# Two transformer blocks in full precision: the second block's mixing reordered with two heads in step, its context turned earlier, tables loaded ahead

## The chip, the core and the metric

One core of one Trainium2 chip runs the whole kernel. Its engines work side by side and wait for each other by semaphores: TensorE (PE, with its weight loads, PEld), VectorE (DVE), ScalarE (ACT), GpSimd (POOL) and SyncE (SP); the last two mainly issue DMAs here. The metric is the device time of one execution in microseconds (us); lower is better.

## The reference, cut to what matters

Two blocks of depth 2 follow each other on 256 latent tokens of width 1024. Each has its own 256 context tokens; the second block gets its own, `ctx_2`, so that these don't depend on the first block. The first block has feed-forwards, attentions and layer norms; its last feed-forward works on the 256 latent tokens alone. The second block's layer is (latent and context in layer 0; in layer 1 context only gives keys and values):

```
h  = rms_norm(x) * (1 + scale) + shift          # 512 tokens
p  = h @ w_in                                    # u, v, f, q-latent, kv-latent, k-rope: 1216 columns
ya = gelu(u) * (w_sgu @ (rms_norm(gelu(v)) * sgu_norm) + b_sgu)      # chunks of 128 tokens
yb = real(fft2(f))                                                    # over tokens and 64 channels
q  = rms_norm(rms_norm(pq) * q_lora_norm @ w_uq) * q_norm             # 4 heads of 128 + 64
k, v = from rms_norm(pkv) * kv_lora_norm @ w_ukv; k = rms_norm([k, k_rope]) * k_norm
q, k = rope(q), rope(k)                          # latent tokens
yc = softmax(q k^T / sqrt(192)) v                # latent: 512 keys; context: 256 keys
x  = x + gate * (concat(ya, yb, yc) @ w_out)
x  = x + gate2 * expert_choice_moe(...)          # 16 experts, 32 tokens each
```

## The kernel before, in words

Activations lie with channels on the 128 partitions and tokens along the free axis: `h` is 8 tiles of 128 x 512, latent tokens first. Large products are made of three products of reduced-precision halves: ACT copies a weight tile from `raw` to `whi` (L1308), DVE subtracts to get `wlo` (L1721), activations are split the same way into `xhi` and `xlo`, and PE multiplies hi by hi, lo by hi and hi by lo (L686 to L688, and L716 to L718 for the first three weight tiles of a stage, which take input tiles as they come). SP fetches weight tiles ("units") of 512 KB into a ring of four; ACT and DVE split three ahead. Small products are in full precision (`small_product`), two instructions each. Every engine runs its instructions in the order in which they are written; PSUM banks 0 to 7 are handed over by `acquire`, `filled`, `evacuated`. Banks 0 to 3 serve the products with units, 4 to 7 the rest.

The first block ends with layer 1's window attention (two heads in step; scores L906, turning of probabilities L933), an output projection, a layer norm and a feed-forward on 256 tokens. `layer_norm` and `inverse_root` sum squares on PE (L767), take the root on ACT (L1392, `square_root`) and the reciprocal on DVE (L1839), and spread it by PE (L774). The feed-forward's input goes DVE (L1869), ACT (L1356, L1361), DVE (L1756), the last two over all 512 columns. POOL streams modulation weights (`ride`, L2361) one feed-forward after the other, then waits until block 1 is done, loads `ctx_2` (L2401) and the small weights of the second block (L2411). PE turns `ctx_2` (L1036), DVE copies it to `h` (L2135).

A layer of the second block: squares (L1563), root, scaling, then ten tiles of input products in the order u, v, f, q, kv, k-rope, whose results ACT moves to `px` with gelu or copy (L1589). Then all the small work, one piece after the other on PE: sums of squares (L1065), turning of w_sgu (L1071), Fourier over channels (L1078), one reciprocal for three norms (L2164), Fourier over tokens (`fourier`, L1049), turning of v (L1094), the gate with its bias as a one-row product (L1103, L1104; DVE L2196), queries, keys, values (through L1023), sums over heads (L1023, `sq`), reciprocals (`inverse`, L2141), spreading over heads, head norms on DVE (L2221 to L2230), rotation (L1990 to L1994). Then `attend` takes one head and 128 query tokens at a time: 16 items in layer 0, 8 in layer 1. For an item PE makes scores (L800), DVE the maximum (L1900), ACT exp (L1412), DVE the reciprocal and the scaling (L1908, L1911), PE turns the probabilities (L809), ACT moves them (L1420), and PE multiplies with the values (L820) once a pair of items is done. Scores are two items ahead. Output products, router (L1654) and experts follow; the expert ring of six 2 MB slots lies over the unit ring and the input tiles, and SP fills it only once all output products are done.

## Time and profile before

| | |
|---|---|
| three executions, us | 3224.4, 3234.5 (median), 3239.0 |
| profiled execution, us | 3243.6 |
| its span | 3241.9 |
| its mean granted TensorE clock | 0.921 |
| PE busy | 2847.9 us, 88% |
| DVE busy | 1308.9 us, 40% |
| ACT busy | 902.4 us, 28% |
| HBM read | 524.62 MB, 162 GB/s over the span |

The span is what the profile covers; 1.7 us lie around it. Times in rows are microseconds from its start. A group's row gives out<-in, shapes, count, busy time and mean ns, then the engine's idle time before and who ended it. PEclk is the granted share of TensorE's full clock.

### The profile page before, as it was taken

The page shows a single profiled execution, that of the slowest core. Times are in us where ns is not written, and L with a number is a line of the kernel's source. Part 1 is how long each engine was busy: PE and PEld are TensorE (multiplying, and loading weights), DVE is VectorE, ACT ScalarE, POOL GpSimd, SP SyncE. Part 2 cuts the span into 40 slices and gives each one's busy share as a digit, 9 for nine tenths or more (in the row PEclk, how much of TensorE's full clock was granted, in tenths as well). Part 3 has the DMA queues.
Part 4 walks back from the last instruction along what each step waited for, and adds up shares of the span by engine and source line. Part 5 has one row for each costly group of instructions (what it writes and reads, how often), then busy time and mean ns, then how long its engine had stood idle before and what let it go on. Part 6 is the DMA issues. An engine that isn't in the chain of part 4 may idle for free.

```text
span 3241.9 us, 42169 instructions
## 1 busy us (share of the span) xinstructions
PE 2847.9 (88%) x15238; PEld 1964.7 (61%) x15238; DVE 1308.9 (40%) x2192; ACT 902.4 (28%) x1418; POOL 193.9 (6%) x338
## 2 busy tenths in 40 slices
PE   5999989988999998999988799788786987867998
PEld 4777766656777776777765589763363333625333
DVE  4333354445333355333365556634223233443112
ACT  2222244443222224222244344342122101422100
POOL 0100003210110100101100000000000000000000
PEclk9999989998999998999989899888587998888999
DMA  7755223322655734747531266420011998203997
GB/s 264 234 165 175 74 82 79 77 54 78 220 192 153 226 93 133 227 123 222 178 88 51 65 201 179 143 82 1 0 71 81 414 427 317 72 0 136 399 427 302
DMA packets 428442, 527.30 MB, mean 163 GB/s; under 512 B 29702, under 2 KB 382468, under 8 KB 415908
## 3 DMA queue, kind: packets, MB, share of 16 engines
q1 hardware_dynamic: 392884, 399.73, 35.7%
q0 software_dynamic: 35440, 125.98, 12.1%
q8 instruction: 75, 1.23, 0.2%
q14 instruction: 43, 0.35, 0.0%
HBM read 524.62 MB, written 1.05 MB: 162 GB/s over the span
## 4 chain that ended last, share of the span: by engine, by line
PE 78%; DMA 8%; DVE 7%; ACT 4%; issue 2%; SPq 1%; DVEq 0%; ACTq 0%; POOL 0%; POOLq 0%
PE bank L686 15%; PE bank L687 15%; PE bank L688 14%; DMA experts<-in_w_up 7%; PE bank L1213 5%; PE bank L651 3%; PE bank L1023 3%; PE bank L800 2%; PE bank L1239 1%; PE bank L882 1%; PE bank L767 1%; PE bank L716 1%; PE bank L883 1%; PE bank L884 1%; PE bank L717 1%
## 5 line engine op out<-in xcount | busy, mean ns | idle before, releaser
L1721 DVE TENSOR_TENSOR wlo<-raw,whi 128x1024 fp32r<-128x1024 f32 x392 | 478.3, 1223 | 502.6 <-ACT whi L1308 477.2
L1308 ACT ACTIVATE whi<-raw 128x1024 fp32r<-128x1024 f32 x392 | 413.5, 1057 | 633.6 <-PE bank L688 578.3
L686 PE MATMUL bank<-xhi,whi 128*128 128x512 f32 (+1 forms) x1568 | 579.0, 369 | 5.0 <-DVE xlo L1923 3.3
L687 PE MATMUL bank<-xlo,whi 128*128 128x512 f32 (+1 forms) x1568 | 566.5, 361 | 0.0
L688 PE MATMUL bank<-xhi,wlo 128*128 128x512 f32 (+1 forms) x1568 | 564.5, 360 | 0.0
L686 PEld LDWEIGHTS bank<-xhi,whi 128*128 128x128 f32 x1568 | 297.0, 189 | 94.7 <-issue 51.8
L688 PEld LDWEIGHTS bank<-xhi,wlo 128*128 128x128 f32 x1568 | 297.4, 190 | 46.7
L687 PEld LDWEIGHTS bank<-xlo,whi 128*128 128x128 f32 x1568 | 297.4, 190 | 40.8
L686 PE MATMUL bank<-hhi,whi 128*128 128x512 f32 (+1 forms) x704 | 260.8, 371 | 21.5 <-DVE hlo L1828 21.5
L1213 PE MATMUL bank<-experts,xsT 128*64 128x512 f32 (+1 forms) x1024 | 236.1, 612 | 27.5 <-DMA experts<-in_w_up 25.2
L687 PE MATMUL bank<-hlo,whi 128*128 128x512 f32 (+1 forms) x704 | 259.2, 368 | 0.0
L688 PE MATMUL bank<-hhi,wlo 128*128 128x512 f32 (+1 forms) x704 | 259.1, 368 | 0.0
L1213 PEld LDWEIGHTS bank<-experts,xsT 128*64 128x64 f32 (+1 forms) x1024 | 75.3, 126 | 177.8 <-issue 177.8
L1821 DVE TENSOR_TENSOR tmp<-tmp,bank 128x512 f32<-128x512 f32 (+1 forms) x88 | 54.6, 621 | 272.6 <-ACT tmp L1382 272.6
L686 PEld LDWEIGHTS bank<-hhi,whi 128*128 128x128 f32 x704 | 135.7, 193 | 44.1 <-issue 23.0
L687 PEld LDWEIGHTS bank<-hlo,whi 128*128 128x128 f32 x704 | 136.0, 193 | 21.1
L688 PEld LDWEIGHTS bank<-hhi,wlo 128*128 128x128 f32 x704 | 135.6, 193 | 21.7
L1792 DVE SCALAR_TENSOR_TENSOR h<-bank,mod,h 128x256 f32 (+1 forms) x160 | 77.5, 484 | 163.1 <-PE bank L688 147.9
L1382 ACT ACTIVATE tmp<-bank 128x512 f32<-128x512 f32 (+1 forms) x88 | 47.8, 544 | 333.8 <-PE bank L688 333.8
L1239 PE MATMUL bank<-experts,hidT 128*32 128x512 f32 x768 | 114.8, 598 | 11.0 <-ACT hidT L1687 11.0
L651 PE MATMUL bank<-mod_ring,cond 128*32 128x256 f32 x1792 | 120.6, 385 | 0.6 <-DMA mod_ring<-in_w_ada 0.5
L2316 DVE TENSOR_TENSOR hid<-sg,bank 64x512 f32<-64x512 f32 (+1 forms) x32 | 22.0, 687 | 242.4 <-ACT sg L1682 242.4
(289 smaller groups left out, 3435.4 us busy)
## 6 DMA issues: line engine op xcount, KB each, us to landing
raw<-in_ffn_w_in SPq DMA_DIRECT2D x176, 512.0 KB, 4.3
mod_ring<-in_w_mod POOLq DMA_DIRECT2D x128, 512.0 KB, 4.3
experts<-in_w_gate SPq DMA_DIRECT2D x32, 2048.0 KB, 16.9
experts<-in_w_up SPq DMA_DIRECT2D x32, 2048.0 KB, 21.3
experts<-in_w_down SPq DMA_DIRECT2D x32, 2048.0 KB, 16.9
mod_ring<-in_w_ada POOLq DMA_DIRECT2D x96, 512.0 KB, 4.8
raw<-in_ffn_w_out SPq DMA_DIRECT2D x64, 384.0 KB, 3.3
raw<-in_ffn_w_out SPq DMA_DIRECT2D x64, 320.0 KB, 3.0
```

What stands on the lines that cost most here:

```text
L651: pe.matmul(bank[b][32 * q:32 * q + 32, 0:MOD_COLS // 4], cond[:, k, :], four[:, q], start=(k == 0), stop=(k == KD - 1), skip_group_check= ...
L686: pe.matmul(o, wh, hi[:, k0 + k, cols], start=(first and k == 0), stop=False)
L687: pe.matmul(o, wh, lo[:, k0 + k, cols], start=False, stop=False)
L688: mm = pe.matmul(o, wl, hi[:, k0 + k, cols], start=False, stop=(last and k == kt - 1))
L800: mm = pe.matmul(bank[b][:, 0:nk], lhs, rhs, start=(j == 0), stop=(j == len(ops) - 1))
L1023: mm = pe.matmul(bank[b][rows, o], lhs, rhs, start=(j == 0), stop=(j == len(pairs) - 1), skip_group_check=True)
L1213: mm = pe.matmul(bank[i][part * HD:part * HD + ns, :], xsT[:, j, 2 * p + i, 0:ns], experts[slots[part]][:, j * 512:(j + 1) * 512], start=( ...
L1239: mm = pe.matmul(bank[2 + half][t * CAP:(t + 1) * CAP, :], hidT[:, j, i * HD + g * CAP:i * HD + (g + 1) * CAP], experts[slots[i]][:, j * D ...
L1308: act.activation(whi[:, slot, :], raw[:, slot, :], ACT.Copy).then_inc(*n.mark("hi_ready"))
L1721: dve.tensor_tensor(wlo[:, slot, :], raw[:, slot, :], whi[:, slot, :].bitcast(F32), ALU.subtract)\
L1792: dve.scalar_tensor_tensor(x, bank[b][:, gc].unsqueeze(1), mod[:, MOD_IN[m], ds(gate * KD + k, 1), g], x, ALU.mult, ALU.add)\
L1821: dve.tensor_tensor(tmp[:, 2 + f, cols], tmp[:, f, cols], bank[2 * f + 1][:, cols], ALU.mult)\
```

## The change

- Block 2's ten input tiles come in the order kv, q, q, k-rope, f, f, v, v, u, u (`IN_ORDER`). After the fourth, small work stands between them: latent mean; query products; tile 4; keys and values; query sums; tile 5; key sums, w_sgu turned, query norms spread; tile 6; Fourier over channels, key norms spread; tile 7; rotation; tile 8; v turned; tile 9.
- Queries are made from the latent times its gain without its own norm; the head sums take two more terms (`eps_256`), which put the norm's epsilon in. ACT makes the latents' squares and scaled copies from the bank.
- The gate's norm is a sum along rows on ACT (accumulated squares) and a scaling on DVE when v is moved; the bias comes from a broadcast tile, added on DVE. Gate and Fourier over tokens stand after the first scores.
- Attention takes two heads and 128 query tokens a step: 8 steps in layer 0, 4 in layer 1, with scores in banks 3 and 4, probabilities in 5 and 6, results in 2 and 7; the two heads' 64-row score products stand side by side. Scores are one step ahead.
- `ctx_2` is loaded into `hm`'s free half after block 1's last output projection, ahead of the last modulation weights, and turned in the last feed-forward behind its first four products.
- The last feed-forward's input is copied and split on 256 columns. `table_of` runs a function on one column ahead of the place where its table is wanted. Tables `half0`, `half1`, `mean_192` are 32 wide.

```diff
-    for name, width in (("ident", P), ("mean_d", P), ("mean_256", P), ("mean_128", P), ("mean_192", P),
-                        ("half0", P), ("half1", P), ("ones", P), ("rot", P), ("cos", S),
+    for name, width in (("ident", P), ("mean_d", P), ("eps_256", 32), ("mean_128", P), ("mean_192", 32),
+                        ("half0", 32), ("half1", 32), ("ones", P), ("rot", P), ("cos", S),
...
+    gated = at("gated", [P, 2, 2, P], F32, big + 18 * KB)
...
+        IN_ORDER = (8, 6, 7, 9, 4, 5, 2, 3, 0, 1)
...
+        def mla_steps(ctx_too):
+            for pair in range(MLA_HEADS // 2):
                 for g in range(2 if ctx_too else 1):
                     for tt in range(2):
...
-            return items, pvs, outs, (slice(0, T) if ctx_too else LAT)
+                        yield pair, g, tt, 4 - 2 * g, tt == 1 and g == int(ctx_too)
...
+                            if new_context:
+                                pe.wait_ge(*n.next("ctx_loaded", 2 * 16))
+                                for k in range(KD):
+                                    acquire(4 + k % 2)
+                                    for t in range(2):
+                                        mm = pe.transpose(bank[4 + k % 2][:, t * P:(t + 1) * P], hm[:, 4 * t + k // 2, S + k % 2 * P:S + (k % 2 + 1) * P],
+                                                          tab("ident"))
+                                    mm.then_inc(s[f"bank_ready{4 + k % 2}"], 1)
...
+                def into(idx):
+                    acquire(idx % 4)
+                    product(idx % 4, unit(), KD, 0, xhi, xlo, slice(0, T) if IN_ORDER[idx] >= 8 else cols, True, True)
+                def head_sums(b, terms, c):
+                    for j in range(len(terms(0))):
+                        for hh in range(MLA_HEADS):
+                            lhs, rhs = terms(hh)[j]
+                            mm = pe.matmul(bank[b][32 * hh:32 * hh + 32, c], lhs, rhs, start=(j == 0), stop=(j == len(terms(0)) - 1),
+                                           skip_group_check=True)
+                            if j == len(terms(0)) - 1:
+                                mm.then_inc(s[f"square_sum{hh}"], 1)
+                def spread(side, c):
+                    pe.wait_ge(*n.next("inverse_ready"))
+                    for hh in range(MLA_HEADS):
+                        acquire(4 + hh)
+                        if side == 0 and hh < 2:
+                            pe.sem_inc(s[f"bank_ready{4 + hh}"], 1)
+                        small_product(4 + hh, [(row_of(hh), tmp[:, side, c])], c, acq=False)
+                first_products(range(3), (slice(0, T), cols, cols), input_tiles())
+                into(3)
+                pe.wait_ge(*n.next("small_loaded", 6 * 16))
+                pe.wait_ge(*n.next("squared"))
+                small_product(4, [(tab("mean_128"), px[:, 0, :])])
...
+                into(4)
+                pe.wait_ge(*n.next("kv_ready"))
...
+                pe.wait_ge(*n.next("squared", 9))
                 acquire(4)
-                for part, (tiles, m) in enumerate(((2, "mean_256"), (2, "mean_256"), (1, "mean_128"))):
-                    c = slice(0, T) if part == 2 else cols
-                    for j in range(tiles):
-                        pe.wait_ge(*n.next("squared"))
-                        mm = pe.matmul(bank[4][32 * part:32 * part + 32, c], tab(m)[:, 0:32], sq[:, 2 * part + j, c],
-                                       start=(j == 0), stop=(j == tiles - 1), skip_group_check=True)
-                mm.then_inc(s["bank_ready4"], 1)
+                head_sums(4, lambda hh: [(tab("mean_192"), sq[:, hh, cols]), (tab(f"half{hh % 2}"), sq[:, 4 + hh // 2, cols]),
+                                         (tab("eps_256"), px[:, 2, cols]), (tab("eps_256"), px[:, 3, cols])], cols)
+                into(5)
+                pe.wait_ge(*n.next("squared", 4))
+                acquire(5)
+                head_sums(5, lambda hh: [(tab("mean_192"), sq[:, hh, :]), (tab("half0"), px[:, 1, :])], slice(0, T))
...
+                spread(0, cols)
+                into(6)
+                evacuated(0)
+                evacuated(1)
...
+                spread(1, slice(0, T))
+                into(7)
...
+                into(8)
...
+                def scores(n_):
+                    pair, g, tt, nk, _ = steps[n_]
+                    q, keys = slice((2 * g + tt) * P, (2 * g + tt + 1) * P), slice(T - nk * P, T)
+                    acquire(3)
+                    acquire(4)
+                    for e in range(2):
+                        pe.matmul(bank[3 + e][:, 0:nk * P], qn[:, 2 * pair + e, q], kn[:, 2 * pair + e, keys], start=True, stop=False,
+                                  skip_group_check=True)
+                    for e in range(2):
+                        rows = slice(e * HD, (e + 1) * HD)
+                        pe.matmul(bank[3 + e][:, 0:nk * P], qr[rows, pair, q], kr[rows, pair, keys], start=False, stop=True,
+                                  skip_group_check=True).then_inc(s["bank_ready4" if e else "score_ready"], 1)
...
+                scores(0)
+                fourier(0)
+                fourier(1)
+                gate(0)
+                for n_, (pair, g, tt, nk, last) in enumerate(steps):
+                    for e in range(2):
+                        pe.wait_ge(*n.next("p_ready"))
+                        acquire(5 + e)
+                        for kt in range(nk):
+                            mm = pe.transpose(bank[5 + e][:, kt * P:(kt + 1) * P], prob2[:, e, kt * P:(kt + 1) * P], tab("ident"))
+                        mm.then_inc(s[f"bank_ready{5 + e}"], 1)
+                    if n_ + 1 < len(steps):
+                        scores(n_ + 1)
+                    if n_ == 0 and ctx_too:
+                        gate(1)
+                    if tt:
+                        evacuated(5)
+                        evacuated(6)
+                        if g == 0:
+                            acquire(2)
+                            acquire(7)
...
+            def modulated(m, scale, cols):
+                input_of(h, lambda k, g: mcol(m, scale, k, g), lambda k, g: mb[:, k, g:g + 1], cols)
...
+            def table_of(function):
+                act.activation(small[:, 60:61], eps_rms, function)
...
+                table_of(ACT.Sqrt)
...
+                def into(idx, function=ACT.Copy, scale=1.0, squares=None):
                     units(1)
+                    j, b = IN_ORDER[idx], idx % 4
                     c = cols if j < 8 else slice(0, T)
-                    act.activation(px[:, j, c], bank[j % 4][:, c], ACT.Gelu_apprx_tanh if j < 4 else ACT.Copy)\
-                        .then_inc(*n.mark(f"bank_read{j % 4}"))
-                own()
-                for j, t in enumerate((2, 3, 6, 7, 8)):
-                    c = cols if t < 8 else slice(0, T)
-                    square(j, px[:, t, c], c)
+                    if squares is not None:
+                        act.activation(px[:, squares, c], bank[b][:, c], ACT.Square).then_inc(*n.mark("squared"))
+                    act.activation(kr_raw[:, c] if j == 9 else px[:, j, c], bank[b][:, c], function, scale=scale).then_inc(*n.mark(f"bank_read{b}"))
+                def root(b, j, c, eps):
+                    act.activation(tmp[:, j, c], bank[b][:, c], ACT.Sqrt, bias=eps).then_inc(*n.mark(f"bank_read{b}"))
+                into(0, squares=0)
+                into(1, ACT.Identity, v("qlora", 2 * l, 1), squares=2)
+                into(2, ACT.Identity, v("qlora", 2 * l + 1, 1), squares=3)
+                into(3, squares=1)
                 act.wait_ge(*n.filled(4))
...
+                root(4, 0, slice(0, T), eps_rms)
...
+                act.activation(small[:, 44:44 + len(tts)], small[:, 40:40 + len(tts)], ACT.Sqrt, bias=eps_rms, scale=1 / S).then_inc(*n.mark("gate_root"))
+                table_of(ACT.Exp)
...
+                def head_norms(gain, nope, rope_gain, raw_rope, rope, c):
+                    for hh in range(MLA_HEADS):
+                        rows = slice(hh % 2 * HD, hh % 2 * HD + HD)
+                        b = bank[4 + hh]
+                        dve.wait_ge(*n.filled(4 + hh))
+                        x = nope[:, hh, c]
+                        dve.scalar_tensor_tensor(x, x, v(gain, l, 1), b[:, c], ALU.mult, ALU.mult).then_inc(*n.mark("dve"))
+                        dve.scalar_tensor_tensor(rope[rows, hh // 2, c], raw_rope(hh)[rows, c], v(rope_gain, l, 1)[rows, :], b[rows, c], ALU.mult, ALU.mult)                            .then_inc(*n.mark(f"bank_read{4 + hh}"))
...
+                for n_, (pair, g, tt, nk, last) in enumerate(steps):
+                    for b in (5, 6):
+                        n.next(f"bank_read{b}")
+                    if n_ + 1 < len(steps):
+                        most(n_ + 1)
+                        normalise(n_ + 1)
+                    if n_ < len(tts) // 2:
+                        gate(n_)
...
-            for riders in RIDERS[1:]:
+            for riders in RIDERS[1:3]:
                 ride(riders)
-            pool.wait_ge(*n.next("h_ready", 7))
-            pool.dma_start(xtok[:, 0:2, :], a["ctx_2"][0].rearrange("(t p) d -> p t d", p=P)).then_inc(s["ctx_loaded"], 16)
+            pool.wait_ge(*n.next("h_ready", 5))
+            rows = a["ctx_2"][0].rearrange("(t p) (q c) -> t p q c", p=P, c=S)
+            for t in range(2):
+                pool.dma_start(hm[:, 4 * t:4 * t + 4, CTX], rows[t]).then_inc(s["ctx_loaded"], 16)
+            ride(RIDERS[3])
+            pool.wait_ge(*n.next("h_ready", 2))
```

## Rows read from the trace of the kernel before

**Rows 1.** The chain that ended last, by engine (page, part 4).
```profile
PE 78%; DMA 8%; DVE 7%; ACT 4%; issue 2%; SPq 1%; DVEq 0%; ACTq 0%; POOL 0%; POOLq 0%
```

**Rows 2.** Stretches: us; busy PE, PEld, DVE, ACT, POOL (x count); PEclk, DMA share, GB/s.
```profile
2144.00:2182.00 38.00, 37.87 (x168) 31.02 (x166) 11.04 (x9) 12.24 (x18) 0.00 (x0) 1.00 0.42 120
2182.00:2274.00 92.00, 72.91 (x213) 33.63 (x213) 44.96 (x69) 21.84 (x36) 0.00 (x0) 0.85 0.01 3
2274.00:2372.00 98.00, 76.70 (x160) 39.00 (x160) 21.04 (x52) 21.91 (x53) 0.00 (x0) 0.57 0.00 0
2800.00:2868.00 68.00, 47.76 (x168) 24.70 (x168) 35.97 (x60) 15.54 (x34) 0.00 (x0) 0.87 0.00 0
2868.00:2924.00 56.00, 40.56 (x96) 18.21 (x96) 12.55 (x29) 13.33 (x29) 0.00 (x0) 0.76 0.00 0
1704.00:1801.00 97.00, 78.87 (x456) 52.71 (x456) 57.02 (x135) 46.33 (x95) 0.00 (x0) 0.93 0.18 48
1801.00:1826.00 25.00, 16.41 (x74) 9.36 (x76) 8.78 (x25) 9.46 (x20) 0.00 (x0) 0.67 0.00 0
2206.00:2221.00 15.00, 13.67 (x26) 7.01 (x26) 3.43 (x12) 0.00 (x0) 0.00 (x0) 0.50 0.00 0
```

**Rows 3.** Groups of PE instructions, layer 0's small work; each product is two instructions.
```profile
L1078 PE MATMUL bank<-tables,px 128*128 128x256 f32 x16 | 3.9, 391 | 0.0
...
L1071 PE MATMUL bank<-tables,wsgu 128*128 128x128 f32 x4 | 0.7, 287 | 0.0
...
L1023 PE MATMUL bank<-px,wuq 128*128 128x512 f32 x16 | 7.0, 592 | 0.0
...
L1023 PE MATMUL bank<-px,wukv 128*128 128x512 f32 x8 | 3.9, 618 | 0.0
L1023 PE MATMUL bank<-px,wuq 128*64 128x512 f32 x16 | 3.7, 601 | 0.0
...
L1023 PE MATMUL bank<-sq,tables 128*32 128x512 f32 x16 | 1.9, 598 | 0.0
```

**Rows 4.** The same view, DVE: a reciprocal and a head norm of 512 columns.
```profile
L2141 DVE RECIPROCAL tmp<-tmp 128x512 f32<-128x512 f32 x2 | 6.7, 3353 | 5.7 <-ACT tmp L1571 5.7
...
L2229 DVE SCALAR_TENSOR_TENSOR kn<-kn,vec,bank 128x512 f32<-128x512 f32 x4 | 3.0, 741 | 0.1
```

**Rows 5.** PE's timeline: block 1's last two-headed steps, then layer 0's first score.
```profile
1814.57 1.09 PE L933 MATMUL bank<-tables,probW 128*128 128x128 f32 x8 [0.56 <-DVE probW L2019]
1815.60 1.13 PE L906 MATMUL bank<-kW,qW 64*128 64x512 f32 x4
1820.25 1.97 PE L933 MATMUL bank<-tables,probW 128*128 128x128 f32 x8 [3.53 <-DVE probW L2019]
...
2273.97 2.08 PE L800 MATMUL bank<-kn,qn 128*128 128x512 f32 x2 [3.33 <-DVE kr L1994]
```

**Rows 6.** ACT's table loads before roots: the group, one of them, one root without.
```profile
L1392 ACT ACT_TABLE_LOAD x9 | 11.5, 1283 | 8.7 <-PE bank L767 8.7
...
2424.04 1.28 ACT L1392 ACT_TABLE_LOAD   x1 [0.93 <-PE bank L767]
2425.33 0.37 ACT L1392 ACTIVATE tmp<-bank,small 128x128 f32<-128x128 f32 x1
...
2117.69 0.37 ACT L1392 ACTIVATE tmp<-bank,small 128x128 f32<-128x128 f32 x1 [0.72 <-PE bank L767]
```

**Rows 7.** Timeline: last feed-forward's start, then the second context's way in.
```profile
1867.94 0.55 PE L716 MATMUL bank<-xhi,whi 128*128 128x256 f32 x1 [4.02 <-DVE xlo L1756]
...
1879.00 0.28 PE L718 MATMUL bank<-xhi,wlo 128*128 128x256 f32 x1
...
2101.97 0.70 POOL L2401 DMA_DIRECT2D xtok<-in_ctx  x1 [192.30 <-DVEq L2147]
...
2107.31 4.84 PE L1036 MATMUL bank<-tables,xtok 128*128 128x128 f32 x16 [11.70 <-DMA xtok<-in_ctx]
...
2112.70 4.27 ACT L1563 ACTIVATE hm<-h 128x512 f32<-128x512 f32 x8 [19.34 <-DVEq L2115]
```

583 lines of the change are left out of this document (250 added, 333 removed).

## The prediction

> **What bounds it now.** I read the chain of waits first: TensorE (PE) carries 78% of it, VectorE (DVE) 7% and ScalarE (ACT) 4% [rows 1]. So PE is the bound, but not everywhere for the same reason, and the table of stretches shows where [rows 2]. "Layer" below is the second block's unless said otherwise. In layer 0's input products (2144 to 2182) PE is busy all the time at the upper clock level, 2.4 GHz. From their last product to the first score (2182 to 2274, 92 us) PE is busy for 73 us. In the attention (2274 to 2372, 98 us) it is busy for 77 us, but at a mean granted clock of 0.57, so most of the time it is at the lower level, 1.2 GHz. Layer 1 has the same parts: 68 us of small work, 56 us of attention. From 2372 on output products, routing and experts follow, which the change leaves alone, and whose loads start only behind the output products; so what is saved ahead of them is saved whole. Chain and table together say: 314 us lie in small work and attention, and each idle or slow PE microsecond there counts.
>
> **The sum's clock.** The profiled execution took 3243.6 us; it stands 9.1 us (0.28%) above the median of the three runs, 3234.5. I subtract the sum from the median.
>
> **Small work, layer 0 (92 us now).** After the change the pieces of small work stand between input products, so that ACT's and DVE's steps run under a product of 5.4 us (38 us for seven [rows 2]). What is left is PE's own work, priced at the upper level. A 128x512 product in full precision comes from "px,wukv": 3.9 us for 4, 1.0 each [rows 3]. The latent's mean: 1.0. Query products as before, 7.0 + 3.7. Keys and values 3.9 + 3.9. Query sums: 16 products into four groups of 32 columns; 8 such took 1.9 us [rows 3], so 3.9; key sums 8, 1.9. Turning w_sgu 0.7 for 4 blocks, so the gate's 8 1.5. Spreading two roots over heads, 2 x 4 x 1.0 = 7.8. Fourier's first stage 3.9. Rotation: 4 products of 256 columns, half of that, 1.9. Together 41. The reciprocals (3.35 each) and head norms (eight at 0.74 a side) of DVE [rows 4] have covers: the first reciprocal lies under the query products and one input product (10.7 + 5.4 us), the second under another, the key norms (5.9) under spreading and a product (3.9 + 5.4). The third, behind the key sums, is followed by the query norms: 0.7 + 3.4 + 5.9 = 10 us against 0.7 + 3.9 + 5.4 = 10.0 of PE work, just hidden. For some 15 hand-overs and short falls of the clock (0.93 in the stage of block 1 that is interleaved in the same way, 1704 to 1801 [rows 2]) I add 6. So 92 becomes 47: **-45**. The second Fourier stage and the gate, which stood in the 92, come back in the attention's sum.
>
> **Small work, layer 1 (68 us now).** Queries have 256 columns: 1.0 + 5.4 + 7.8 + 1.9 + 1.9 + 0.7 + 1.9 + 3.9 + 2.0 + 1.9 + 0.7 = 29. The covers are products of half the columns now, some 2.8 us. The chain of reciprocal and query norms (0.7 + 3.4 + 4.0 = 8.1) stands against 5.5 of PE work (0.7 + 1.9 + 2.8, with a short wait): 2.6 show. With 4 for hand-overs: 36. **-32**.
>
> **Attention.** A step turns two heads' probabilities (T), makes the next two scores (S), then waits for reduce, exp, reciprocal and scaling of both. The nearest rows are the two-headed steps of block 1 without products beside them [rows 5]: T 1.1 us at the upper level, 2.0 at the lower; the pair of 64-row score products 1.1 (by T's ratio 2.1 at the lower level), since both heads run side by side; and from the end of S to the next T 3.5 us. S here has in addition two 128-row products, 1.0 each, 2.0 at the lower level (the last line of [rows 5]). So S is 3.0 or 6.1 with 512 keys, half of that with 256, where the wait is 2.6 (shorter reduce, exp and scaling). Layer 0 has 4 steps of each kind. At the upper level: T 6.4, S after the first 15.2, waits 20.9, weighted values beyond their cover 2, tail 3.2, and ahead of them the first scores, two Fourier products and the gate 3.0 + 7.3 + 2 = 12.3 (the Fourier products as the first stage, sixteen of 256 columns), which hide the first wait: 60. At the lower level 94. Block 1's like stretch had 0.67 [rows 2], today's attention 0.57; I take 0.65. PE's part is 38 of the 60, so 38 / 0.65 + 22 = 80 against 98: **-18**. Layer 1, 4 steps of 512 keys: 37 at the upper level, 62 at the lower, PE's part 25; its stage had 0.76, I take 0.7: 48 against 56: **-8**.
>
> **Tables of ACT.** Nine loads stand between the sum of squares and the root. Each costs 1.283 us, and the ACTIVATE starts right at its end (2424.04 + 1.28, 2425.33); the wait ahead is 0.93 instead of 0.72 where nothing is loaded [rows 6]. So 1.5 each, all on the chain: **-13.5**. At 2117.69 the root needs no load after squares, so a square keeps the root's table, and an early load stays good. The Trainium skill (ScalarE: Activation LUTs, What ACT_TABLE_LOAD costs) gives some 2.66 us per switch, a drain included; by it the nine would give 24 instead of 13.5. No row shows that drain; the sum keeps 1.5. The early exp table in the router gains nothing: there ACT's copies, not the logits, are late, and the load comes behind them as before. Loads in the mixing: three before, three after, all beside PE work.
>
> **Second context.** Today its load is issued at 2101.97, lands at 2107.3, and after 4.8 us of turning the squares start at 2112.70 [rows 7]. With it gone they start at about 2102.0: -10.7. The turning moves into a feed-forward in which PE is the bound: 4.8 us, and a first wait of some 1.3 while DVE finishes the hidden tile: +6. The load moves on POOL's queue ahead of the last modulation weights and waits for block 1's last output projection; a whole normalisation and the first four products (11.3 us for three of them, below) lie between it and its use, and it took 5.3. Net **-5**. **256 tokens** in the last feed-forward's input: today ACT sets the pace, 1.5 us a tile, and three products take 11.3 us (1867.94 to 1879.28) [rows 7]; at half the copy PE sets it: **-2**. SP's order of loads costs nothing (0.42 DMA share in that stretch [rows 2]); one more small transfer on POOL hides under the products.
>
> Sum: 45 + 32 + 18 + 8 + 13.5 + 5 + 2 = 123.5. 3234.5 - 123.5 = **3111 us**.
>
> **Rivals.** *The clock stays up.* The attention's PE would be busier and better filled. All else as forecast, 60 instead of 80 and 37 instead of 48: 3080. Against it: PE was busy 91% of 2206 to 2221 at 0.50 [rows 2], and 78% of today's attention at 0.57; for it, 0.93 with products beside. The Trainium skill (TensorE: Matmul & The Clock Gate, What's actually happening) says activity releases the throttle; by that alone this rival would hold, which these rows contradict. Chance 0.1.
> *Attention low, hand-overs long.* Attention at the lower level (+14, +14) or 15 us of uncovered DVE chain: 3140. For it: DVE does reductions, gate, splits and residual parts in one queue, in order, and a late gate delays the next maximum. Chance 0.2.
> *Two heads don't overlap.* If the 64-row pairs run one behind the other as today (S +1.0 a step upper, +2 lower), and the two reductions add fully, 12 steps give back some 20: 3131. Rows 5 speak against. Chance 0.04.
> *Slower.* The interleaved products themselves fall to the lower level because small products between them starve the clock. Layer 0 has 38 + 41 us of such work, layer 1 some 37 + 29; at the lower level all of it doubles, +145, with the attentions' +28: 3284. It turns slower than before once two thirds of that work runs at the lower level. For it 0.50 at 2206 to 2221; against it 0.93 in block 1's like stage and 1.00 at 2144 to 2182 [rows 2]. Chance 0.02.
> The forecast itself has 0.64.
>
> **Numbers.** 0.5% is 16 us, about what a measurement of this kernel tells from no change. All cases but the last lie beyond it on the faster side; 0.02 is left for cases that cancel to within it. The range reaches to the first two rivals and a little past each, for the bounds of the hand-overs: 3075 to 3150.
>
> **Right or wrong by the profile after.** From last input product to first score under 6 us in both layers; input products and small work of layer 0 from start to first score about 105 us; attention of layer 0 near 80 with a clock of 0.6 to 0.7, layer 1 near 48; no load between square sums and root; first squares of the block at once behind the first block; the stages behind the mixing of their old length. Idle PE over 10 us behind DVE in the mixing, or an attention clock outside 0.55 to 0.8, would move the number.

## The result, and the profile after

The changed kernel takes **3075.86 us** (median of 4 runs, 3068.02 to 3079.94), the kernel before 3231.8 in as many (3224.41 to 3238.98): ratio 0.9514, 95% interval 0.9499 to 0.953. That is 156 us less; 3111 was forecast, 123.5 less, and the result lies at the low end of the stated 3075 to 3150. The profiled execution took 3077.4 (span 3075.8, clock 0.941), 166 us less than the profiled one of before, which stood 9 above its median.

The page's chain of the changed kernel, by engine, can't be laid beside [rows 1]: its shares add up to 32% of the span, so most of the time has no link in it.

```profile
PE 20%; DMA 7%; DVE 3%; ACT 2%; issue 0%; SPq 0%; DVEq 0%; ACTq 0%
```

So I compare stretches that begin and end with the same instruction: from root to root of the norms, and inside the second block from the first input product to the first score and from there to the first output product.

| stretch, us | before | after | difference | forecast |
|---|---|---|---|---|
| layer 0: input product to score | 149.7 | 95.5 | -54.2 | -45 |
| layer 0: score to output product | 98.2 | 61.0 | -37.2 | -18 |
| layer 1: input product to score | 105.8 | 68.0 | -37.8 | -32 |
| layer 1: score to output product | 55.9 | 41.1 | -14.8 | -8 |
| last feed-forward of block 1, root to root | 231.68 | 232.98 | +1.3 | +6, -2, -1.5 |
| next norm's root | 24.70 | 14.05 | -10.65 | -10.7 |

The five other root-to-root stretches ahead of the second block's mixing, and between its layers, are 1.3 to 4.0 us shorter each; a table load of 1.5 is gone from every one. The 289.4 us behind the last root are 289.35. Windows of the changed kernel, in the columns of [rows 2]: layer 0's input products and small work, its attention, its output products, then the same of layer 1:

```profile
2124.00:2201.00 77.00, 76.75 (x320) 48.22 (x318) 44.17 (x50) 30.47 (x53) 0.00 (x0) 1.00 0.19 56
2201.00:2261.00 60.00, 47.74 (x226) 31.78 (x224) 26.25 (x64) 25.54 (x62) 0.00 (x0) 0.94 0.03 8
2261.00:2305.00 44.00, 42.76 (x181) 35.22 (x182) 13.59 (x20) 5.24 (x6) 0.00 (x0) 0.96 0.05 12
2661.00:2717.00 56.00, 53.45 (x312) 38.08 (x311) 38.95 (x49) 24.84 (x48) 0.00 (x0) 0.97 0.27 76
2717.00:2757.00 40.00, 32.95 (x133) 20.65 (x131) 16.62 (x38) 16.54 (x36) 0.00 (x0) 0.83 0.10 27
```

In layer 0's interleaved part TensorE is busy 76.75 of 77 us, all of it at the upper level: there is no hand-over to see. The attention, 0.57 and 0.76 before [rows 2], has 0.94 and 0.83. This is the difference to explain. TensorE's timeline of the changed kernel, one two-headed step of layer 0 and the wait on the query norms in layer 1's small work:

```profile
2238.93 1.88 PE L1092 MATMUL bank<-kn,qn 128*128 128x512 f32 x4
2240.74 1.13 PE L1096 MATMUL bank<-kr,qr 64*128 64x512 f32 x4
2245.03 1.09 PE L1132 MATMUL bank<-tables,prob 128*128 128x128 f32 x8 [3.16 <-DVE prob L2210]
...
2699.20 2.04 PE L1065 MATMUL bank<-tables,px 128*128 128x256 f32 x7 [2.22 <-DVE qr L2178]
```

A step's turn is 1.09, its scores 1.88 and 1.13, its wait 3.16: the figures of [rows 5], 3.5 for the wait, carried over, and both heads' 64-row products do run side by side. The wait on the query norms is 2.22 (2.6 forecast).

ScalarE's timeline of the changed kernel: a table loaded by the one-column instruction during a feed-forward, two roots that need no load, and between them the squares of the second block's first norm:

```profile
461.82 1.28 ACT L1397 ACT_TABLE_LOAD   x1 [2.39 <-PE bank L673]
463.12 0.20 ACT L1397 ACTIVATE small<-small 128x1 f32<-128x1 f32 x1
...
2084.14 0.36 ACT L1404 ACTIVATE tmp<-bank,small 64x128 f32<-64x128 f32 x1 [1.56 <-PE bank L761]
...
2092.97 4.27 ACT L1551 ACTIVATE hm<-h 128x512 f32<-128x512 f32 x8 [8.37 <-DVEq L2109]
2098.19 0.37 ACT L1404 ACTIVATE tmp<-bank,small 128x128 f32<-128x128 f32 x1 [0.95 <-PE bank L761]
```

The last of these roots follows its sums by 0.95 without a load (0.72 in [rows 6]'s case without one). The squares ahead of it start 8.8 us behind the root of 2084.14; before, with the load and the turning of the context in between [rows 7], it was 19.7.

### The profile page after: what moved, and what is told of

It is laid out like the page before. It is cut to its first block and busy times, and to the rows that moved or that the text cites. A ratio compares the mean times of both kernels' runs of the same rounds, so it can differ in the third digit from the quotient of the medians.

```text
span 3075.8 us, 42149 instructions
## 1 busy us (share of the span) xinstructions
PE 2755.1 (90%) x15242; PEld 1933.2 (63%) x15242; DVE 1298.0 (42%) x2168; ACT 898.2 (29%) x1437; POOL 195.9 (6%) x341
## 5 line engine op out<-in xcount | busy, mean ns | idle before, releaser
L672 PEld LDWEIGHTS bank<-xlo,whi 128*128 128x128 f32 x1568 | 297.1, 189 | 41.1 <-issue 0.7
```

The source lines that it names most:

```text
L672: pe.matmul(o, wh, lo[:, k0 + k, cols], start=False, stop=False)
```

## The experiments

Where a median or an interval is given, a kernel ran four times; every other kernel ran once, and its stretches are read from that run's trace. The waits of a stretch repeat from trace to trace, the granted clock doesn't: four kernels with the changed kernel's own attention, or nearly (the changed one and e4, e11 and e12 below) have the same waits to 0.1 us, but in layer 0 60.2 to 62.7 us at 0.94 to 0.88, and in layer 1 38.7 to 41.1 us at 0.91 to 0.83. A difference of that size in one stretch says nothing.

**What holds the clock.** Two theories to begin with: the stretch keeps the level at which it is entered ("entry": it now comes straight from 77 us without a pause), or the steps themselves are filled well enough to hold or regain the upper level ("filling").

*A pause ahead of the attention.* VectorE works 10 us that nobody needs, and the first score waits for it.

```diff
@@ PE, second block @@
+                pe.wait_ge(*n.next("idled"))
                 scores(0)
@@ DVE, ahead of most(0) @@
+                for _ in range(3):
+                    own()
+                    dve.reciprocal(tmp[:, 0, :], tmp[:, 0, :]).then_inc(*n.mark("dve"))
+                own()
+                dve.sem_inc(*n.mark("idled"))
```

> The changed kernel, with TensorE held idle for some 10 us ahead of the first scores of both layers (three more reciprocals on a free tile of DVE, for which PE waits). In the changed kernel layer 0's attention took 60 us at a granted clock of 0.94, where I forecast 80 at 0.65. Theory 'entry': the level at which the attention is entered is kept, since its own work neither raises nor lowers it; then layer 0's attention runs at 0.5 to 0.65 and takes over 85 us, layer 1's over 50. Theory 'filling': two heads in step fill the array well enough to hold and to regain the upper level; then the clock is back within some 10 us and the attention takes 62 to 70 us at over 0.8.

*Dense products ahead of the one-headed attention of the kernel before.*

```diff
+                for r_ in range(48):
+                    pe.matmul(bank[0][:, :], xhi[:, 4 + r_ % 4, 0:P], xhi[:, 4 + r_ % 4, :], start=True, stop=True, skip_group_check=True)
                 attend(mla_plan(ctx_too), BLOCK2)
```

> The kernel before, with 48 dense products of 128x512 (split inputs, into a free bank, their result unused) between the rotation and the first scores. Its attention took 98 us at 0.57. Theory 'entry': the one-headed attention is entered at the upper level and keeps it: layer 0's attention over 0.85 and 70 to 78 us. Theory 'filling': one head at a time can't hold the level: below 0.7 and over 90 us, as before.

*The two heads' score products one behind the other.*

```diff
                     for e in range(2):
                         pe.matmul(bank[3 + e][:, 0:nk * P], qn[:, 2 * pair + e, q], kn[:, 2 * pair + e, keys], start=True, stop=False,
                                   skip_group_check=True)
-                    for e in range(2):
                         rows = slice(e * HD, (e + 1) * HD)
                         pe.matmul(bank[3 + e][:, 0:nk * P], qr[rows, pair, q], kr[rows, pair, keys], start=False, stop=True,
                                   skip_group_check=True).then_inc(s["bank_ready4" if e else "score_ready"], 1)
```

> The changed kernel, with each head's 64-row score product right behind its 128-row product, so that the two heads' 64-row products no longer stand side by side. 'Filling': the half-empty array costs the level: clock below 0.75, layer 0's attention over 72 us. 'Entry': the level stays over 0.88; a step's products grow by 1.0 us with 512 keys and 0.5 with 256, and the first head's maximum starts earlier by nearly as much: 58 to 64 us.

Windows of layer 0's attention, first score to first output product, in these three kernels:

```profile
2206.20:2272.60 66.40, 52.96 (x225) 34.19 (x225) 27.18 (x66) 23.13 (x57) 0.00 (x0) 0.83 0.00 1
```
```profile
2279.30:2360.90 81.60, 60.02 (x161) 30.17 (x159) 21.29 (x53) 21.92 (x53) 0.00 (x0) 0.75 0.00 1
```
```profile
2200.80:2271.30 70.50, 60.46 (x225) 35.41 (x225) 27.20 (x66) 26.86 (x62) 0.00 (x0) 0.88 0.02 7
```

After a pause of 10.3 us the two-headed attention takes 5.4 us more, and in layer 1, after 11.4, half a us more (3101.56 in all, of which 22 are the pauses themselves). It starts at 0.50 and is back at the upper level within 5 us, so "entry" falls. But it comes back in the 18 us of first scores, Fourier products and gate that stand ahead of the first turn; whether the steps alone would have brought it back, this run doesn't show.

The one-headed attention entered at the upper level takes 81.6 us at 0.75 instead of 98.2 (layer 1 51.9 instead of 55.9; 3240.18 in all, with some 9 us of dense products in each layer). It doesn't keep the level: the clock falls within 7 us, and then alternates to the end. The first four stretches of 10 us:

```profile
2279.30:2289.30 10.00, 7.12 (x20) 2.87 (x19) 3.11 (x7) 2.72 (x7) 0.00 (x0) 0.83 0.00 0
2289.30:2299.30 10.00, 8.83 (x18) 4.09 (x17) 2.15 (x6) 2.32 (x6) 0.00 (x0) 0.50 0.01 2
2299.30:2309.30 10.00, 6.14 (x24) 3.23 (x23) 3.11 (x7) 2.92 (x7) 0.00 (x0) 0.99 0.00 0
2309.30:2319.30 10.00, 8.83 (x19) 4.09 (x20) 2.15 (x6) 2.32 (x6) 0.00 (x0) 0.53 0.00 1
```

It is up for some 10 of every 20 us, in the kernel before for some 3.4 of every 24 (slices below). So the same steps, with waits of the same 1.2 to 2.3 us, ran in two different patterns. Neither theory forecast that, and what picks the pattern isn't shown.

Heads apart cost 9.5 us in layer 0 and 7 in layer 1 by these two traces (clock 0.88 and 0.79), 13 in the whole (3089.16): about what the rival "two heads don't overlap" would have given back. Its waits are shorter than the changed kernel's (7.7 against 11.1 us in layer 0), and still its clock is no higher.

**Longer waits.** One more reciprocal in each step's chain, of 256 columns, then of 512.

```diff
                     own()
+                    dve.reciprocal(tmp[:, 0, 0:256], tmp[:, 0, 0:256]).then_inc(*n.mark("dve"))
+                    own()
                     dve.reciprocal(total, total).then_inc(*n.mark("dve"))
```

> The changed kernel with one more VectorE instruction in each two-headed attention step, a reciprocal of 256 columns ahead of the one of the two sums. By half of the 3.35 us that 512 columns took it is worth 1.7 us, all of it in the chain scores, maximum, exponential, scaling, turn, so TensorE's wait ahead of each turn grows from 3.2 to about 4.8 us, in 8 steps of the first layer and 4 of the second. Theory 'the clock hangs on how much of a step TensorE stands still': the attention of the first layer (61.0 us from the first score to the output products in the changed kernel) pays 8 x 1.7 = 14 us for the waits, to 75 us, and then more because the granted clock of the stretch falls from 0.94 towards the 0.57 that the one-headed steps had: 82 to 95 us at a clock under 0.8. Theory 'the clock hangs on what filled the time ahead of the attention': the clock stays above 0.9 and it takes 75 us. Second layer: 41.1 us becomes 48 us without a fall of the clock and over 52 us with one.

> The same with a reciprocal of 512 columns, 3.35 us in each step: TensorE's wait ahead of each turn would be some 6.5 us. Without a change of the clock the attention of the first layer takes 61 + 27 = 88 us; where the clock hangs on how much of a step TensorE stands still it is at its lower level for most of the stretch (granted clock under 0.65) and takes 105 to 120 us, the products of a step (4 us at the upper level) taking twice as long. Second layer: 41 + 13 = 54 us without, 60 to 68 us with.

```profile
2196.10:2273.20 77.10, 53.68 (x226) 33.65 (x224) 41.22 (x74) 26.70 (x62) 0.00 (x0) 0.85 0.02 6
```
```profile
2199.70:2291.90 92.20, 57.39 (x225) 36.57 (x223) 53.85 (x74) 27.04 (x62) 0.00 (x0) 0.76 0.02 5
```

61.0 became 77.1 and 92.2 us (3093.02 and 3117.16 in all). The waits for the scaled probabilities grew from 11.1 to 21.0 and 32.5 us; the busy time, for the same products, from 47.6 to 53.7 and 57.4. The fall I expected did not come: in layer 0 the clock gives way by 0.09 a dose, not by half, and in layer 1 (46.8 and 53.0 us) not at all: 0.85 and 0.84, after 0.83. And it shows that the idle share does not set it: here TensorE stands still 38% of the time at 0.76, in the kernel before 22% of the time at 0.57 [rows 2].

**Filled pauses in the kernel before.** If it isn't how much TensorE stands still, it may be how the one-headed steps are cut up. Slices of 4 us show it, kernel before, then the changed kernel:

```profile
2292.00:2296.00 4.00, 3.65 (x6) 1.32 (x6) 0.29 (x1) 0.62 (x3) 0.00 (x0) 0.50 0.00 0
2296.00:2300.00 4.00, 4.00 (x9) 2.70 (x9) 1.21 (x3) 0.78 (x2) 0.00 (x0) 0.50 0.00 0
2300.00:2304.00 4.00, 2.97 (x8) 1.11 (x6) 0.85 (x2) 0.65 (x2) 0.00 (x0) 0.86 0.00 0
2304.00:2308.00 4.00, 3.46 (x9) 2.16 (x10) 0.78 (x2) 1.11 (x3) 0.00 (x0) 0.57 0.00 0
2308.00:2312.00 4.00, 1.71 (x5) 0.81 (x4) 1.47 (x4) 1.16 (x3) 0.00 (x0) 0.50 0.00 0
```
```profile
2213.00:2217.00 4.00, 4.00 (x27) 1.88 (x25) 0.77 (x2) 1.15 (x3) 0.00 (x0) 1.00 0.00 0
2217.00:2221.00 4.00, 1.86 (x12) 1.75 (x9) 2.93 (x9) 2.00 (x5) 0.00 (x0) 0.78 0.00 0
2221.00:2225.00 4.00, 4.00 (x17) 2.75 (x16) 1.47 (x4) 1.61 (x5) 0.00 (x0) 0.79 0.00 0
2225.00:2229.00 4.00, 4.00 (x22) 2.99 (x21) 2.67 (x9) 0.73 (x3) 0.00 (x0) 1.00 0.00 0
2229.00:2233.00 4.00, 1.72 (x9) 1.05 (x8) 2.84 (x7) 2.79 (x8) 0.00 (x0) 1.00 0.00 0
```

In the kernel before, runs of products of 3.1, 10.6 and 5.1 us follow one another with pauses of 1.2 to 2.3 between, three times over. The clock rises near the end of the 10.6, a pause of 1.6 follows, and soon it is down again: it is up where there is least to gain. Each product then takes twice as long, and the pattern repeats. The changed kernel falls behind the pause of 2.1 us at 2217 and is back within 6 us. It stays up through the next three, one of 3.16 included, and falls again for 3 us behind the one of 2.3 at 2253. So I put one and then two products that nobody reads into each pause of the kernel before:

```diff
                 for m, it in enumerate(items):
-                    pe.wait_ge(*n.next("p_ready"))
                     acquire(6)
+                    if m:
+                        for _ in range(1):
+                            pe.matmul(bank[6][:, :], kn[:, 0, 0:P], kn[:, 0, :], start=True, stop=True, skip_group_check=True)
+                    pe.wait_ge(*n.next("p_ready"))
```

> The kernel before, with one product of 512 columns that nobody reads ahead of each wait for scaled probabilities in its one-headed attention steps (15 of them in the first layer, 7 in the second). Such a product takes 0.94 us at the upper level of the clock and 1.9 at the lower (two instructions of 947 ns in the stretch whose clock was 0.57), and the waits that it stands in are 1.2 to 2.3 us. Theory 'the pauses of the one-headed steps hold the clock down': the granted clock of the first layer's attention rises from 0.57 to 0.75 or more, and it takes less than the 98.2 us of before although it computes more: 80 to 92 us. Rival, by which the pauses are not what holds it down (the many short products are): the clock stays at 0.5 to 0.6, and the time stays at 98 or grows by up to 15 x 0.9 us to 112.

> The same with two such products in each wait, 1.9 us at the upper level of the clock. 'Pauses hold the clock down': hardly a pause over 1 us is left, the granted clock of the first layer's attention is 0.9 or more, and it takes 74 to 84 us against 98.2 (16 steps of 0.55 us of turn, 1.4 of scores and 0.8 of weighted values on average, and 1.9 of filling). That would say how the 37 us that the changed attention gained are split: 15 to 24 of them the clock's, the rest the waits'. Rival: the clock stays under 0.65 and the attention takes 105 to 125 us.

```profile
2269.10:2343.20 74.10, 63.74 (x191) 29.86 (x191) 21.27 (x53) 21.92 (x53) 0.00 (x0) 0.91 0.00 0
```
```profile
2274.20:2355.00 80.80, 75.09 (x220) 36.03 (x220) 21.18 (x53) 21.93 (x53) 0.00 (x0) 0.92 0.00 1
```

With one such product the attention of layer 0 takes 74.1 us instead of 98.2, though TensorE computes 17 us of products more; the whole kernel 3208.92 against 3228.14 beside it. The clock goes from 0.57 to 0.91. Layer 1 goes from 55.9 to 49.4 us, at 0.87. With two, the filling (30 us) is in the way and nothing more is gained: 80.8, and 3217.55 in all. This is the experiment that bears most on the cause: of the 37 us, 24 can be had without two heads, by the clock alone; the two-headed form is another 13 shorter (74.1 to 61.0). TensorE's useful products are busy 46.6 and 47.6 us in the two; waits and filling together take 27.5 us there, the waits 13.5 here. The filling does two things at once, though: it closes part of the pause and puts one more wide product into each step. No run parts the two.

By the Trainium skill (TensorE: Matmul & The Clock Gate, HAM oscillation — how this bites in real kernels) a wait for DMA in each step of a loop makes the next step start at the lower level again, and the cure is to do the steps without waits between. The slices of the kernel before agree (0.50, then 0.86, then 0.50), with waits for a softmax in the DMA's place, and so does the filled pause (0.91). But not every pause does it: of the changed kernel's three of 3.16 us, the clock stays at 1.00 through the one in layer 0 and is at 0.50 behind both in layer 1.

**Parts of the change.**

*Fourier products ahead of the first scores*, so that nothing covers the first softmax.

```diff
-                scores(0)
                 fourier(0)
                 fourier(1)
+                scores(0)
```

> The changed kernel with both halves of the Fourier products issued ahead of the first scores on TensorE instead of behind them. They cover the first wait for a softmax in the changed kernel (7.17 us of products behind the scores). Expected: TensorE stands still for one whole softmax of 3.2 to 3.6 us in each layer, +3.5 us in each, +7 in all, with the clock of the stretches as they are (0.94 and 0.83). Rival, by which the clock is what matters: a pause right at the start of the attention costs a stretch at the lower level, another 3 to 6 us in each layer, +13 to +19 in all.

From input product to output product layer 0 takes 162.6 us against 156.5, layer 1 111.3 against 109.1; 3085.25 in all. That is 6.1 and 2.2. TensorE's wait is there in both, 2.9 us. The other 3 in layer 0 may be the clock (0.89 over the attention), but e11, which has no such wait, had 0.88, so this doesn't tell for the rival.

*A product's cover taken away* (TensorE's part of the edit; ScalarE's and VectorE's queues follow it).

```diff
                 into(4)
+                into(5)
...
-                into(5)
                 pe.wait_ge(*n.next("squared", 4))
```

> The changed kernel with the products into(5) of the second block's input moved from behind the squares' sums of the queries to ahead of them, right behind into(4), on all engines; nothing else. ScalarE's squares then have no products ahead of them on TensorE. If the order of the small work is what won 54 us in the first layer and 38 in the second, through cover of each wait by a projection, then taking this one cover must show as a wait of about 3 us on TensorE in each layer (first product to first score 95.5 to 98.5 to 101 us, and 68 to 71 to 73), +6 to +8 in all. Rival, 'the clock's upper level was the gain and single waits are absorbed': under 1 us.

The group of the query sums in layer 0's small work, which had no idle time in the changed kernel:

```profile
L1004 PE MATMUL bank<-sq,tables 128*32 128x512 f32 x24 | 3.0, 600 | 3.1 <-ACT sq L1555 3.1
```

Layer 0's part grew from 95.5 to 98.9, layer 1's from 68.0 to 69.6; 3078.78 in all. The wait appears where it was forecast in both layers, 3.1 and 2.8 us; in layer 1 the stretch gets back 1.2 of it elsewhere, and I can't place them. At this place a product's cover is what the order is worth; the other covers were not taken away one by one.

*Tables loaded late again:* `table_of` does nothing.

```diff
             def table_of(function):
-                act.activation(small[:, 60:61], eps_rms, function)
+                pass
```

> The changed kernel without the early table loads, everything else kept. By my sum each of nine loads costs 1.5 us on the path (1.28 and a longer wait): 13.5 slower, ratio to the changed kernel 1.0044. By the Trainium skill's 2.66 us a switch (ScalarE: Activation LUTs, What ACT_TABLE_LOAD costs): 24 slower, 1.008. Rival: the loads go to other places on the path, and it is under 6.

3090.78 us (3084.82 to 3092.1), ratio to before 0.9561 (0.9529 to 0.9593) against 0.9514: 15 us, 1.7 a load, by the medians; by the two intervals it could be 4 to 27. The nine loads are back at the roots:

```profile
L1404 ACT ACT_TABLE_LOAD x9 | 11.5, 1283 | 8.1 <-PE bank L761 8.1
```

The medians alone can't tell the load's 11.5 from more, the traces can: VectorE waits 38.9 us for the ten roots here, 29.0 in the changed kernel and 39.2 before, so the nine loads are worth 10 there. The root starts 0.02 us behind each load's end, and ScalarE's wait ahead of a load (8.1 for nine) is no longer than ahead of a root without one (9.8 for ten in the changed kernel). By an estimate from the Trainium skill's figure (ScalarE: Activation LUTs, What ACT_TABLE_LOAD costs) the nine would have been 24; the traces don't agree.

*The second context late again*, loaded and turned where it was.

```diff
-                up_down(cols, RIDERS[2 * l + 1], new_context=l > 0)
+                up_down(cols, RIDERS[2 * l + 1], new_context=False)
@@ ahead of the second block, as in the kernel before @@
+            pe.wait_ge(*n.next("ctx_loaded", 16))
+            for k in range(KD):
+                b = 4 + k % 2
+                acquire(b)
+                for t in range(2):
+                    mm = pe.transpose(bank[b][:, t * P:(t + 1) * P], xtok[:, t, k * P:(k + 1) * P], tab("ident"))
+                mm.then_inc(s[f"bank_ready{b}"], 1)
```

> The changed kernel with the second context's load and its turning at the old place, behind the last feed-forward of the first layer. The stretch between the two norms' roots goes back from 14.05 to the 24.7 us of before (+10.65), and the feed-forward ahead of it loses what the turning cost there, 6 us by the prediction, of which the comparison showed 1.3 (232.98 against 231.68) beside 2 us that the narrower columns should give. Expected: +5 by the prediction's sum; by the comparison of the two traces +9 (10.65 less 1 to 3). Chances about even for 4 to 7 and 8 to 11.

3080.32 us (3070.52 to 3082.51), ratio 0.9533 (0.951 to 0.9556): 4.5 more by the medians, less than the intervals can tell, and so read from the stretches: the norm goes from 14.05 to 24.90, the feed-forward from 232.98 to 225.81. Turning inside the feed-forward costs 7.2, outside it 10.85: net 3.7. It also parts what the comparison had mixed: the feed-forward without turning went from 231.68 to 225.81; with 1.5 for the table, the 256 columns have 4.4.

**Towards a faster version.** Each head scaled behind its own exponential; then the same with a filled pause in each step; then that with filled pauses in the norms.

```diff
@@ e8, e13, e14: DVE @@
                     for e in range(2):
                         dve.wait_ge(*n.next(f"bank_read{3 + e}"))
-                    own()
-                    dve.reciprocal(total, total).then_inc(*n.mark("dve"))
-                    own()
-                    for e in range(2):
+                        own()
+                        dve.reciprocal(total, total).then_inc(*n.mark("dve"))
+                        own()
@@ e13, e14: PE, in front of the turn @@
+                        if n_ and not e:
+                            fill(5, kn[:, 0, :], 1)
@@ e14: PE, layer_norm and inverse_root @@
+                fill(4, tab("dft_n", 0, 2 * S), 2)
                 pe.wait_ge(*n.next("h_ready"))
...
+                fill(4, tab("dft_n", 0, 2 * S), 1)
                 pe.wait_ge(*n.next("root_ready"))
...
                 mm.then_inc(s["bank_ready4"], 1)
+                fill(5, tab("dft_n", 0, 2 * S), 4)
```

> The changed kernel, where VectorE takes the reciprocal of each head's sum and scales its probabilities right behind that head's own exponential, instead of one reciprocal of both sums behind the second exponential. One reciprocal of 0.17 us is added to each step, and the first head's scaling (0.48 us) runs beside the second head's exponential. The chain to the turn gets shorter by 0.5 us less at most 0.2 for the added reciprocal: 0.3 to 0.5 us in each of 12 steps, 4 us in all (1 to 6), 0.1% of the time, at the edge of what the rounds tell. Rival: TensorE's first four transposes wait for both heads, or VectorE's added instruction lies on the chain as well: no gain, or 1 to 2 us slower.

3066.57 us (3062.11 to 3067.21), ratio 0.9481 (0.9465 to 0.9497). TensorE's waits for the scaled probabilities fell from 11.1 to 7.5 us in layer 0 and from 6.3 to 4.7 in layer 1, more than expected. The attentions took 60.2 (0.91) and 37.7 us (0.91 instead of 0.83), 4.2 less together, the number expected; but most of it is layer 1's clock, which differs by as much in equal code. The medians differ by 9; the rest has no place in the steps.

> The changed kernel with each head scaled behind its own exponential (as in e8_scale_each) and one product of 512 columns that nobody reads ahead of TensorE's wait for the scaled probabilities, in each two-headed step but the first. At the upper level it takes 0.94 us, less than every pause it stands in but one (1.2 to 3.2 us in the changed kernel). Theory 'the pauses rule the clock': the granted clock of the two stretches goes from 0.91 and 0.91 in e8 (0.94 and 0.83 in the changed kernel) to 0.95 or more, and the attention takes 56 to 59 us in the first layer and 36 to 37.5 in the second, 2 to 5 us less than e8 in all. Rival: the steps are bound by the softmax and not by the clock now, so nothing is gained (within 1 us of 60.2 and 37.7), or the filling delays the turn by up to 0.9 us in each step, 8 us in all.

```profile
2198.00:2256.90 58.90, 52.61 (x239) 32.08 (x237) 29.12 (x74) 26.83 (x62) 0.00 (x0) 0.97 0.03 8
```

Clock 0.97 and 0.95, 58.9 and 37.5 us: 1.5 less than in e8, short of the 2 to 5; the whole, 3067.36 (ratio 0.9489, 0.9458 to 0.952), shows no gain. The two-headed steps had little left to win from the clock.

> The same, and in each of the ten norms the same kind of product that nobody reads: two ahead of the mean's product, one ahead of the broadcast of the root, four behind it, where TensorE stood still for 2.5, 1.65 and 4.3 us at the norm ahead of 1235 us (clock at 0.5 from 1217 to 1237). Theory 'pauses take the clock down, and it comes back some microseconds after they end, wherever they lie': the norm's own products (2.1, 4.8 and 2.1 us) and the first 4 us behind them run at the upper level, which saves up to 4.4 + 2 us in each; but what then ends the squares' and the root's stages is ScalarE and VectorE, so half of that: 3 to 5 us in each of 10 norms, 25 to 50 us in all against e13. Rival: the norms are bound by ScalarE and VectorE alone, and filled products delay the mean's and the root's (up to 1.9 us each at the lower level): 0 to 30 us slower.

3048.88 us (3038.37 to 3049.64), ratio **0.9421** (0.9388 to 0.9454): 18.5 less than e13, 27 less than the changed kernel, the fastest of all. The two attentions have 2.6 of it; the rest would be some 1.6 for each of the ten norms, below the 3 to 5 expected. It isn't even: from root to root the stretches of the first block are between 2.8 us longer and 3.8 shorter than in e13. Around the norm between block 1's two layers, the kernel of e8, then this one:

```profile
1217.00:1237.00 20.00, 12.53 (x83) 6.81 (x84) 13.19 (x26) 12.37 (x24) 0.00 (x0) 0.50 0.00 1
```
```profile
1220.00:1232.00 12.00, 10.56 (x40) 6.67 (x40) 8.69 (x14) 8.86 (x18) 0.00 (x0) 1.00 0.00 0
```

And TensorE's timeline of this kernel in that norm (L757 is the filling):

```profile
1210.03 1.88 PE L757 MATMUL bank<-tables 128*128 128x512 f32 x4
1212.70 1.13 PE L786 MATMUL bank<-tmp,tables 128*128 128x512 f32 x2 [0.79 <-DVEq L1872]
1215.36 4.52 PE L766 MATMUL bank<-hm,tables 128*32 128x128 f32 x64 [1.53 <-ACT hm L1422]
1219.81 1.12 PE L757 MATMUL bank<-tables 128*128 128x512 f32 x2
1221.53 1.16 PE L774 MATMUL bank<-tmp,tables 128*128 128x128 f32 x8 [0.59 <-DVE tmp L1879]
```

The mean's product and the broadcast now take half as long (1.13 and 1.16, against 2.08 each in e8), but in front of the squares TensorE still waits 1.53 for ScalarE, unfilled, and there the clock falls once: the 64 small products take 4.52 (4.75 in e8). At three of the ten norms, those at 786, 1843 and 2759 us, it doesn't fall at all. I expected those to gain too; a filling at that place wasn't tried.

## Why the prediction missed

- **Attention, the step that failed.** "Block 1's like stretch had 0.67 [rows 2], today's attention 0.57; I take 0.65. PE's part is 38 of the 60, so 38 / 0.65 + 22 = 80". It ran at 0.94 and took 61.0; layer 1, taken at 0.7 for 48, ran at 0.83 and took 41.1. With the measured clocks the same sum gives 38 / 0.94 + 22 = 62 and 25 / 0.83 + 12 = 42, so its other terms held; only the clock was wrong. (Its 94 for the lower level is a slip: by its own parts it is 38 / 0.5 + 22 = 98.) I treated the clock as a property of the kind of work and took it from the nearest rows. The filled pauses show that it changes when the pauses in the steps do, and the change altered those; that this is also how the two-headed steps came to 0.94 is argued from them, not shown by a run of its own. 26 us of the miss stand here, 15 in the small work; together 41 of the 42.5 by which the two profiled executions differ more than forecast (35 by result and forecast, 3111 against 3075.86, since the profiled one of before lay above its median). The rival "The clock stays up", 3080 with a chance of 0.1, is what came in the attention. That the whole lies so near its number is in part luck: it had nothing of the 15 us of the small work, took the attentions 5 us shorter than they came, and the profiled execution of before stood 9 us above its median.
- **Small work.** PE's own sum held, and so did the covers. The 6 and 4 us for hand-overs and falls of the clock were not there: 76.75 of 77 us busy at 1.00. These 77 us, filled by products, had no hand-overs to price. Some 3 of the 9 us missed in layer 0 I can't place. In layer 1 the one forecast stall was 2.22 for 2.6, and the 6 us missed are the 4 and some 2 more.
- **Tables:** 13.5 forecast, 15 by medians, 10 in VectorE's waits. The 0.2 a load for a longer wait ahead of it doesn't show in the traces. **Second context:** 5 forecast, 3.7 by stretches, 4.5 by medians; its turning costs 7.2, not 6. **256 tokens:** 2 forecast, 4.4 measured. Sized within 4 us each.
- **Two heads side by side** is worth 9.5 and 7 us by one trace, 16.5 in all, and 13 by the whole; the rival gave it 20.
- **The stages behind the mixing** kept their length, as forecast: 289.4 and 289.35 behind the last root.
- **The slower rival** (interleaved products at the lower level) had no place: 1.00 and 0.97 where it wanted 0.5.

What takes the clock down and what brings it back stays open. A pause of 2.1 us was followed by a fall at 2217, one of 3.16 at 2242 was not, and the same 3.16 in layer 1 was, twice; the one-headed steps ran in two patterns by what stood ahead of them; equal code had 0.88 to 0.94. So neither a pause's length nor the share of idle time forecasts it here.

## What to carry to other kernels

When a change alters where TensorE pauses, don't carry a stretch's granted clock over as if it belonged to that kind of work: price the stretch at both levels and give each end a real chance. Where short steps wait on a softmax or a norm and the slices show the clock rising only just before the next pause, filling the pause with a product that nobody reads is a cheap test, and may be a gain in itself (24 us of 98 here), as long as the filling is shorter than the pause. Read waits and clock apart: the waits of a trace repeat, its clock may not. Small work between products that don't depend on it cost its own time here and nothing for hand-overs, as long as the product was longer than the chain it covered; in layer 1, where it was not, 2.2 us showed.

## Not expected of the hardware

- More work in less time: 15 useless products in a stretch of 98 us shortened it to 74 by taking the clock from 0.57 to 0.91.
- More idle time at a higher clock: 35 idle us of 92 at 0.76 in the two-headed steps, against 21 of 98 at 0.57 in the one-headed.
- The same one-headed steps with the same waits took 98.2 us at 0.57 and, with dense products ahead of them, 81.6 at 0.75, up to the end of the stretch.
- Round the norm at 1225 us of e8 the clock is at its lower level for 20 us (0.50 from 1217 to 1237), through pauses of 2.5, 1.5, 1.6 and 4.3 us; with the first and the last two filled it is at 1.00 for the norm's second half. With all ten norms so filled the kernel is 18.5 us faster.
